# Four more norms sum their squares in pairs, after the high halves of their chunks

## What is computed

```python
def rmsnorm(x, g):
    xf = x.astype(jnp.float32)
    y = xf * lax.rsqrt(jnp.mean(xf * xf, axis=-1, keepdims=True) + EPS)
    return (y * g.astype(jnp.float32)).astype(x.dtype)

x = x + memory_cross_attention(rmsnorm(x, norm_xattn_g[layer]), mem_n, ...)
x = x + swiglu(rmsnorm(x, norm_ffn_g[layer]), ffn_w_gate_up[layer], ffn_w_down[layer])
```

## Time and profile before

| what | value |
|---|---|
| runs | 4165.9 us median of 3 (4156.64 to 4167.36) |
| profiled execution | 4161.18 us, span of its instructions 4159.4 us |
| mean granted TensorE clock | 0.952 |
| TensorE busy | 3829.6 us, 92% |
| VectorE busy | 2068.1 us, 50% |
| ScalarE busy | 1096.8 us, 26% |
| L1017, sums of separate squares (norms of width 1024 and two smaller) | 296 records |
| L1674, separate squares of X | 32, median 0.63 us |
| L1683, pair squares | 44, about 1.05 us |
| L2181, adds of pairs | 32, 1.22 us |

### The profile page before, as it was taken

One profiled execution on the slowest core, in us unless ns is written; L12 is line 12 of the kernel. 1 busy time (PEld: TensorE's weight loads), 2 busy tenths in 40 slices (PEclk: granted clock), 3 DMA queues, 4 the chain that ended last, 5 costly groups with the idle time before them and its releaser, 6 DMA issues.

```text
span 4159.4 us, 42350 instructions
## 1 busy us (share of the span) xinstructions
PE 3829.6 (92%) x17182; PEld 3073.3 (74%) x17182; DVE 2068.1 (50%) x2589; ACT 1096.8 (26%) x1218; POOL 48.0 (1%) x65
## 2 busy tenths in 40 slices
PE   8889999978979998999998979999999998979998
PEld 6677888745758887888775757887888775857886
DVE  4555444363455434453656565444443656565433
ACT  2232222133332222222242312222222243312221
POOL 0000000000000000000000000000000000000000
PEclk9899999978999998999999989999999999989999
DMA  3122222210212221222312112222222312112221
GB/s 123 65 71 81 101 96 89 72 41 1 85 54 101 101 91 61 101 88 96 118 61 91 61 56 86 101 96 87 100 93 89 130 61 92 62 51 87 95 96 66
DMA packets 66781, 342.88 MB, mean 82 GB/s; under 512 B 23524, under 2 KB 23524, under 8 KB 30816
## 3 DMA queue, kind: packets, MB, share of 16 engines
q1 hardware_dynamic: 60864, 303.19, 20.9%
q0 software_dynamic: 5792, 37.92, 2.4%
HBM read 324.31 MB, written 16.78 MB: 82 GB/s over the span
## 4 chain that ended last, share of the span: by engine, by line
PE 83%; DVE 11%; ACT 2%; issue 2%; DMA 1%; SPq 0%; DVEq 0%; ACTq 0%
PE ACC L943 24%; PE ACC L945 24%; PE ACC L944 24%; PE MIX L1017 1%; PE ACC L1461 1%; PE ACC L1201 1%; DVE WL L2040 1%; PE MIX L1034 1%; DVE BX L2544 1%; DVE BT L2542 1%; PE ACC L1181 1%; PE MIX L1113 1%; DVE PT L2734 0%; DVE PT L2732 0%; DMA RAW<-wall 0%
## 5 line engine op out<-in xcount | busy, mean ns | idle before, releaser
L943 PE MATMUL ACC<-HH,WH 128*128 128x512 f32 (+1 forms) x3322 | 1317.9, 397 | 92.3 <-issue 27.8
L944 PE MATMUL ACC<-HL,WH 128*128 128x512 f32 (+1 forms) x3322 | 1302.5, 392 | 0.0
L945 PE MATMUL ACC<-HH,WL 128*128 128x512 f32 (+1 forms) x3322 | 1301.1, 392 | 0.0
L2040 DVE TENSOR_TENSOR WL<-RAW,WH 128x2048 fp32r<-128x2048 f32 x292 | 668.2, 2288 | 507.7 <-ACT WH L1620 506.8
L943 PEld LDWEIGHTS ACC<-HH,WH 128*128 128x128 f32 x3322 | 635.3, 191 | 254.0 <-issue 76.6
L944 PEld LDWEIGHTS ACC<-HL,WH 128*128 128x128 f32 x3322 | 636.1, 191 | 131.2 <-issue 3.1
L945 PEld LDWEIGHTS ACC<-HH,WL 128*128 128x128 f32 x3322 | 634.6, 191 | 132.0
L1620 ACT ACTIVATE WH<-RAW 128x2048 fp32r<-128x2048 f32 x292 | 556.2, 1906 | 596.6 <-PE ACC L945 592.2
L945 PE MATMUL ACC<-HIDH,WL 128*128 128x512 f32 x1056 | 421.3, 399 | 0.0
L944 PE MATMUL ACC<-HIDL,WH 128*128 128x512 f32 x1056 | 416.1, 394 | 0.0
L943 PE MATMUL ACC<-HIDH,WH 128*128 128x512 f32 x1056 | 414.0, 392 | 0.0
(11 more groups left out here) (474 smaller groups left out, 3011.7 us busy)
## 6 DMA issues: line engine op xcount, KB each, us to landing
RAW<-wall SPq DMA_DIRECT2D x261, 1024.0 KB, 4.8
RAW<-wall SPq DMA_DIRECT2D x24, 768.0 KB, 4.1
KR<-spectra POOLq DMA_DIRECT2D x4, 2048.0 KB, 9.4
x_kept<-X POOLq DMA_DIRECT2D x2, 2048.0 KB, 6.7
FWK<-mats POOLq DMA_DIRECT2D x4, 1024.0 KB, 5.3
spectra<-SQ POOLq DMA_DIRECT2D x8, 512.0 KB, 2.9
spectra<-T POOLq DMA_DIRECT2D x8, 512.0 KB, 3.5
X<-x_kept POOLq DMA_DIRECT2D x2, 2048.0 KB, 14.6
```

The source lines that it names most:

```text
L943: pe.matmul(out_ap, wh, hh, start=first, stop=False)
L944: pe.matmul(out_ap, wh, hl, start=False, stop=False)
L945: return pe.matmul(out_ap, wl, hh, start=False, stop=last)
L2040: v.tensor_tensor(WL[n % 2][:], RAW[n % 2][:], WH[n % 2][:], ALU.subtract).then_inc(w_lo, 1)
```

## The change

The four norms become `paired` too, and a new mark `alone` says that a late norm has all its squares of its own. On ScalarE the squares of these norms come after the high halves and after the high split of the next weight unit, ahead of the root; for the two xattn norms the first two pairs stay ahead of everything, as X is final there before the memory's linears. VectorE adds pairs 1 and 2 in dve_diag, ahead of add_last, so behind its low split. On TensorE nothing of the norm is ahead of the linear any more: sum_paired stands in the second block ahead of half m = 1, where late_scale was, and late_scale in the middle of that half, 12 matmuls on. The norms with own == 2 and the Hyena norms are as they were.

```diff
--- before.py
+++ after.py
@@ -146,7 +146,8 @@
         st.next_unit = u
         st.u0, st.b0, st.h0, st.nrm, st.ffn = u, b, h, norms, ffns
         st.sq0, st.su0, st.sa0 = squared, summed, added
-        st.paired = st.kind in ("norm", "rms") and (st.own == 2 and st.src == "X" or st.src == "HY")
+        st.paired = st.kind in ("norm", "rms") and st.src in ("X", "HY")
+        st.alone = st.late and st.own == st.n
         st.nth = seen.get(st.kind, 0)
         seen[st.kind] = st.nth + 1
         if st.kind == "linear":
@@ -988,8 +989,10 @@
                             else:
                                 for m in range(1 if st.half and isinstance(i, int) and i * bpp + j == st.nb - 1 else 2):
                                     if second_block and m == 1:
-                                        late_scale(st.norm)
+                                        sum_paired(st.norm) if st.norm.alone else late_scale(st.norm)
                                     for k in ks:
+                                        if second_block and m == 1 and k == KD // 2 and st.norm.alone:
+                                            late_scale(st.norm)
                                         if m == 0 and src_h is HH and not st.whole:
                                             pe.wait_ge(h_ready, st.hin + k + 1)
                                         if m == 0 and src_h is HIDH:
@@ -1682,7 +1685,7 @@
                 src = {"X": X, "HY": HY}[st.src]
                 act.activation((SQB if k else SQ)[:], src[:, st.c0 + 2 * k:st.c0 + 2 * k + 2, :], ACT.Square).then_inc(sq_ready, 1)
 
-            def act_squares(st):
+            def act_squares(st, first=None, end=None):
                 if st.gain == "final":
                     act.wait_ge(par2_landed, 32)
                 if st.gain == "ffn1n0":
@@ -1694,7 +1697,7 @@
                 else:
                     act.wait_ge(block_done, st.b0 if st.gain[:5] != "xattn" else st.b0 - 4)
                 if st.paired:
-                    for k in range((st.n - st.own) // 2, st.n // 2):
+                    for k in range((st.n - st.own) // 2 if first is None else first, st.n // 2 if end is None else end):
                         square_pair(st, k)
                 else:
                     for c in range(st.n):
@@ -1710,14 +1713,18 @@
                     act_root(st)
                     hi_chunks(st.h0, range(st.d0, st.d0 + st.n))
                     return
-                if st.own == st.n:
-                    act_squares(st)
+                ahead = 2 if st.gain[:5] == "xattn" else 0
+                if ahead:
+                    act_squares(st, 0, ahead)
                 if st.u0:
                     act.wait_ge(unit_done, st.u0)
                 hi_chunks(st.h0, range(st.n), first=st.early)
-                if st.own < st.n:
+                if st.alone:
+                    split_hi(st.u0 + 1, 0, 0)
+                    act_squares(st, ahead, st.n // 2)
+                else:
                     act_squares(st)
-                split_hi(st.u0 + 1, 0, 0)
+                    split_hi(st.u0 + 1, 0, 0)
                 act_root(st)
 
             def act_rms(st):
@@ -2188,6 +2195,9 @@
 
             def dve_diag(st):
 
+                if st.alone:
+                    for k in range(1, st.n // 2 - 1):
+                        add_pair(st, k)
                 if st.paired:
                     add_last(st)
                 v.wait_ge(root_ready, st.nrm + 1)
```

## The result

The changed kernel takes 4138.5 us (median of 13, 4135.5 to 4155.6) against 4165.8 (median of 13, 4156.6 to 4168.3) for the kernel before, run beside it: ratio 0.9949, 95% interval 0.9938 to 0.9960. Forecast were 4157 and a range down to 4149, so the gain is 21 us by the ratio (27 by the medians), where 8.65 were worked out. The profiled execution took 4137.25 us with a span of 4135.5 and a mean clock of 0.954; before it was 4161.18, 4159.4 and 0.952. On the page TensorE, shown busy for 3829.6 us before, now has

The account below looks back on a forecast made before the run. TensorE, busy 92% of the span, was taken as the bound. Gains of 0.15, 4.3, 2.7 and 1.5 us at four norms made 8.65, from a median of 4165.9 to 4157 us; range 4149 to 4168.

Parts of the forecast that it names:

- The clock takes part of that back: Step: half clock lasts until 39.2 in mix0 and 1626.4 in ffn1n0; one slow stretch costs 1.6 us in each xattn opening.
- A: The opening at mix0, at the start of the kernel; forecast gain 0.15 us.
- D: The opening at ffn1n0; forecast gain 1.5 us, after 1.6 off for a new slow stretch.
- B: The opening at xattn0; forecast gain 4.3 us, from 5.1 at the second XQ eviction less 0.8 in the scores.
- C: The opening at xattn1; forecast gain 2.7 us, from 3.5 at the second XQ eviction less 0.8 in the scores.
- First matmuls: Each opening's linear starts 1.9 us after T, at 21.5 in mix0; 10.0 us earlier there, 12.5 in ffn1n0.
- sum_paired and 12 matmuls, 3.85: In block 1 of each opening, late_scale comes 3.85 us later within the block, behind sum_paired (1.13) and 12 matmuls (2.72).
- The chain that feeds the sums: Squares, adds and fold on ScalarE and VectorE end 0.4 us before TensorE needs them at xattn0, so cost nothing.
- Waits before block 2: TensorE's wait for VectorE's WL split grows to 4.6 us in mix0 and about 3.7 in ffn1n0.
- Rival 1: Mild clock: rises at the same moments as before, no slow stretch behind new waits; 14.4 us, median 4151.5, chance 0.19.
- rival 2: The whole earlier start is kept at all four openings: 37 us, median 4129, chance 0.03.
- Rivals 3 and 4: More half clock in the openings, or TensorE waiting mid block for squares and adds; median 4168 each, together 0.16.

Follow-up runs that it names:

- warm_before: Kernel before, with unused wide matmuls added on TensorE ahead of the sums, 8 in mix0 and 20 in ffn1n0: 4164.6 us, ratio 0.9992.
- only_ad: Kernel before with only mix0 and ffn1n0 changed, the two xattn norms keeping eight single squares ahead: 4150.0 us, ratio 0.9971.
- only_bc: Kernel before with only xattn0 and xattn1 changed, mix0 and ffn1n0 left as they were: 4149.9 us, ratio 0.9976.
- pairs_first: Changed kernel, but all four pair squares stay ahead of the high halves and the adds ahead of T: 4183.0 us, ratio 1.0033.
- split_ahead: Changed kernel with both splits of the opening's third weight unit moved ahead of block 0's eviction behind late norms: 4112.2 us, ratio 0.9869.
- again: The changed kernel run again with no edit: 4136.5 us, ratio 0.9932.
- warm_after: Changed kernel with unused wide matmuls added ahead of block 0 in mix0 and ffn1n0: 4141.0 us, ratio 0.9945.
- scale_mid: Changed kernel with sum_paired put back between the blocks and late_scale ahead of half m = 1: 4158.9 us, ratio 0.9992.
- none_ahead: Changed kernel without the two pair squares that the xattn norms have ahead: 4135.1 us, one run.

## Why the prediction was wrong

**The step that failed** is "*The clock takes part of that back*". I read that the clock rose 18.0 us after the first sum in A and 19 in D, and took TensorE's first work of any kind as the start of that time. The rise goes with the first wide matmul of the linear ("pace changes" is the start of the first matmul whose next one lies closer than 0.427):

| kernel, place | ahead of it | first wide | pace changes | us |
|---|---|---|---|---|
| before A | 13.8 us of sums | 31.53 | 35.94 | 4.4 |
| before B | 10.2 us of sums | 240.36 | 244.35 | 4.0 |
| before C | 8.6 us of sums | 1131.56 | 1135.11 | 3.6 |
| before D | 13.8 us of sums | 1621.07 | 1626.77, a start later than the prediction read | 5.7 |
| after A | nothing | 21.40 | 25.38 | 4.0 |
| after D | 8.49 us idle | 1595.72 | 1598.85 | 3.1 |
| warm_before A | 8 wide, then 13.65 us of sums | 34.24 | 39.94 | 5.7 |
| warm_before D | 20 wide, then sums | 1630.87 | 1634.0 | 3.1 |

The first four rows were in the trace that I had; A and D were read from their sums, B and C not held against them:

```profile
230.33 10.17 PE L1017 MATMUL MIX<-ONES,SQ 128*128 128x1 f32 x64
...
244.35 0.41 PE L943 MATMUL ACC<-HH,WH 128*128 128x512 f32 x1
...
1131.56 0.77 PE L943 MATMUL ACC<-HH,WH 128*128 128x512 f32 x1
...
1135.11 0.47 PE L945 MATMUL ACC<-HH,WL 128*128 128x512 f32 x1
```

Counted from the first sum (in C at 1123.00) the pace changed after 14.0 us in B and 12.1 in C, so a constant 18 us was already refuted there. (18.0 in A and some 19 in D was the length of the sums, the same in both, plus a few us.)

What the step cost: in A I took 41.5 slow matmuls, there were 9 to 10, so block 1 began at 34.3 instead of 40.7. In D the distance from first matmul to late_scale was 21.7 us (1617.4 - 1595.7) instead of 28.6. Late_scale came 6.6 us earlier than forecast in A and 6.7 us earlier against what enters D: **13.3 us**, more than the whole difference between 21.0 at the four places and 8.65. B and C gave 1.6 less than forecast, and 0.7 came between A's RS and B.

**Point by point, the rest.**
- *First matmuls*: 21.40 for 21.5. In B T began at 223.82 and the matmul at 225.90, 2.1 us for 1.9. In D the start moved 12.4 beyond what entered (25.35 - 12.98), for 12.5. Right.
- *sum_paired and 12 matmuls, 3.85*: 3.67 in A (43.42 - 39.75) and in B (247.62 - 243.95). Right. With it A closes: 10.13 earlier start, 0.3 from a slow stretch of 4.0 for 4.4, less 3.67, is 6.76; measured at RS 6.74. So does D: 12.4 earlier start, 1.1 from a slow stretch of 3.1 for 5.7, less 3.67, is 9.8, as measured at RS (22.80 - 12.98). That 1.1 is luck: in the change run again D's slow stretch was 3.6, in only_ad's D 4.4.
- *No wait at late_scale*: none in A to D. The margin of 0.3 us held.
- *The chain that feeds the sums*: the fold in B ends at 243.31 (242.62 + 0.69), TensorE is there at 243.95, hidden by 0.64 for 0.4. In C block 0 had no slow stretch and TensorE waited 0.87 for the 1.1 that the text names for this case; the clock then fell for 3.4 us, which it doesn't name. So late_scale came 1.2 later than forecast and the XQ eviction moved by 2.3 for 3.5; C came to 2.2 for 2.7 only because the scores' cost of 0.8 hardly showed behind attention (0.1). In the change run again it was 5.3, so this place varies most.
- *Waits before block 2*: 4.68 and 3.66 for 4.6 and 3.7, each with slow matmuls behind it (51.89 to 55.9; 1626.33 to 1629.7). D lost 1.6 by that, from 22.80 ahead at RS to 21.20. Right.
- *B*: the XQ eviction moved by 5.0 for 5.1. The scores lost 1.69 (5.41 - 3.72) for 0.8: the whole slow stretch, not half, and behind attention it was still missing (4.96 less 1.69 is 3.3, measured 3.2).
- *Rival 1* let the clock rise at the same moments as before, which was too late as well; *rival 2*, the whole earlier start, is what A and D did but for the 3.67 us of the later scale and D's new slow stretch. I had written against it that "the clock is low in A and D": low, but not for long. Its 0.03 was far too small.
- *Rivals 3 and 4*: 3 did not come. 4 came as a wait of 0.87 in C.

The Trainium skill ("TensorE: Matmul & The Clock Gate", section "HAM oscillation — how this bites in real kernels") says of its example that each burst behind a wait starts at the lower clock. That agrees with A (slow at once at 51.89) and not with B and D, where the first matmuls were fast and the clock fell 1.0 and 1.5 us later (225.90 to 226.94, 1624.84 to 1626.33), nor with C's opening, where no slow stretch followed a wait of 2.85 us; B's and C's waits are shorter than those of the example. It was no error to weigh it: the new waits before block 2 did cost a slow stretch.

**Left open.** In the after trace 2.9 us of the lead come where nothing was edited, 2.7 in only_bc and 8 of pairs_first's loss too. I haven't shown a cause. Nor is it shown why the pace changes 2.7 us after the first wide matmul in one trace and 6.1 in another, nor what in the tiny sums it is that leaves the clock low: no run here changes their width, their number or their pace singly.

## What to carry to other kernels

Ask of each thing ahead of a linear's first matmul whether that matmul reads it; a sum whose result is wanted a block later belongs behind the operands, and pairing its squares while they stayed ahead made this kernel slower. When the clock is to be forecast, tabulate every place in the trace where the pace changes before taking a distance from one: all rows have to fit the same origin. Once a scale comes earlier, look at what is queued behind it: here moving one weight split ahead of the eviction brought as much again as the change.

## What the hardware showed that I had not expected

- The tiny sums, 64 records back to back with TensorE shown busy throughout, neither raised the clock nor kept it in any of these runs. It fell 3.8 us into them in B (230.33 to 234.1), 5.4 us in C (1123.00 to 1128.4) and 1.8 us in warm_before's D (1618.84 to 1620.6), and stayed low for the 13.4 us up to the linear in the kernel before's D. In all 16 openings with them, over five kernels, the linear's first matmuls were slow.
- From there the pace rose 3.1 to 5.7 us after the first wide matmul, after idling and after sums alike (eight cases above; 2.7 in only_ad's A and 6.1 in only_bc's and split_ahead's A are the ends over all runs).
- The length of a wait alone doesn't decide whether a slow stretch follows. A wait of 0.87 us in C (with 0.9 us of tiny sums right behind it) had one, the same wait of 0.85 us in the change run again had none, nor had that of 0.95 us at 1647.64. In the openings of B and C TensorE waits 2.85 us in both: in B the clock fell about 1 us into the linear in every trace with that wait, in C in none of after, again, only_bc, warm_after, scale_mid and none_ahead.
- At the start of the span the granted clock reads 1.00 (the third figure from the end of this stretch of the after trace) although its matmuls lie 0.427 apart, as the slow ones of D at 0.50 do; there the distance of the starts is what tells the level.

```profile
21.40:25.40 4.00, 4.00 (x10) 3.17 (x11) 3.89 (x8) 2.11 (x4) 0.00 (x0) 1.00 0.58 242
```
